# Expert products of a diffusion backbone step: gated rows turned by transposing DMAs instead of TensorE, the second product four quarters behind the first

## The reference, cut to what matters

```python
D_MODEL = 1024
N_EXPERTS = 8
TOP_K = 2
EXPERT_FF = 1024
# FFN_l, odd l: top-2-of-8 SwiGLU experts; for each chosen expert e of a token
#   y += gate[e] * ((silu(h @ w1[e]) * (h @ w3[e])) @ w2[e])
# x = LayerNorm(alpha * x + gate2 * FFN_l(x * (1 + scale2) + shift2))
```

## Time and profile before

| | us |
|---|---|
| median of 3 executions | 2330.24 (2324.44 to 2332.24) |
| the profiled execution | 2327.33 |
| its span, first to last instruction | 2325.5 |
| expert part, first `up` to last `down` | 1735.7 to 2289.2 |

### The profile page before, as it was taken

How to read it: one execution, slowest core, us unless ns; L and a number is a source line. 1 busy time by engine, 2 the same in 40 slices (tenths; PEclk the granted TensorE clock), 3 DMA queues, 4 the chain that set the end, 5 groups by cost and what they waited for, 6 DMA issues and landing times.

```text
span 2325.5 us, 54083 instructions
## 1 busy us (share of the span) xinstructions
PE 2102.1 (90%) x22914; PEld 1290.5 (55%) x22914; DVE 1440.9 (62%) x1790; ACT 1268.3 (55%) x1652; POOL 751.1 (32%) x545
## 2 busy tenths in 40 slices
PE   4999787978989999999899878878969999999998
PEld 3666456855565555555667558744644444444443
DVE  3362665668262121215547667586379999999997
ACT  3533554556444242424544675465278777777773
POOL 0322215443314343433232226433122333333332
PEclk8999899988999999999999999998979999999999
DMA  9443681020212222134331000020286779993106
GB/s 291 139 136 104 218 275 45 4 59 4 77 54 76 87 70 93 61 101 114 120 111 56 3 11 3 8 55 23 73 290 199 236 236 315 300 342 109 37 20 234
DMA packets 246504, 278.45 MB, mean 120 GB/s; under 512 B 61346, under 2 KB 221966, under 8 KB 246160
## 3 DMA queue, kind: packets, MB, share of 16 engines
q1 hardware_dynamic: 237200, 252.51, 34.6%
q0 software_dynamic: 5984, 20.97, 2.4%
q10 hardware_dynamic: 3103, 1.85, 0.3%
HBM read 360.50 MB, written 29.11 MB: 168 GB/s over the span
## 4 chain that ended last, share of the span: by engine, by line
PE 75%; DVE 9%; ACT 8%; issue 3%; DMA 2%; POOL 2%; SPq 1%; DVEq 0%; ACTq 0%; POOLq 0%
PE ps L2332 74%; DVE arena L1693 1%; ACT mix L1476 1%; DVE arena L1697 1%; DMA wbuf<-in_w_mod 1%; DVE small L1921 1%; DVE mix L1693 1%; SPq L731 1%; DMA const<-in_w_mod 1%; PE ps L3099 1%; DVE hT L1693 1%; ACT arena L1186 1%; ACT hT L1482 1%; POOL extra L922 1%; DVE const L1693 1%
## 5 line engine op out<-in xcount | busy, mean ns | idle before, releaser
L2332 PE MATMUL ps<-hT,mix 128*128 128x512 f16 (+2 forms) x3024 | 376.7, 287 | 24.8 <-DVE hT L1693 11.8
L2332 PE MATMUL ps<-w,xgT 128*128 128x512 f16 x1632 | 365.1, 380 | 4.0 <-DVE w L2239 4.0
L2332 PEld LDWEIGHTS ps<-hT,mix 128*128 128x128 f16 x3024 | 227.1, 99 | 172.7 <-issue 21.8
L2239 DVE SCALAR_TENSOR_TENSOR w<-wst,w 128x2048 f16<-128x2048 f32 x136 | 312.2, 2334 | 5.9 <-ACT w L1573 5.9
L1049 POOL TENSOR_TENSOR a<-aval,a 128x256 f16<-128x256 f32 x68 | 163.4, 2402 | 360.6 <-ACT a L1617 360.6
L2332 PEld LDWEIGHTS ps<-w,xgT 128*128 128x128 f16 x1632 | 157.3, 98 | 182.3 <-ACT xgT L1587 4.2
L1573 ACT ACTIVATE w<-wst 128x2048 f16<-128x2048 f32 x136 | 251.7, 1900 | 2.2 <-DMA xs_rows<-htok,slot_i 2.1
L2332 PE MATMUL ps<-mix 128*128 128x512 f16 (+5 forms) x1856 | 204.0, 287 | 7.2 <-ACT mix L1267 5.7
L2332 PE MATMUL ps<-hT,arena 128*128 128x128 f16 (+1 forms) x1440 | 199.4, 299 | 0.0
L2332 PE MATMUL ps<-w2m,aT 128*128 128x512 f16 x816 | 188.9, 382 | 3.1 <-DVE aT L2266 3.1
L2245 DVE SCALAR_TENSOR_TENSOR w2m<-wst,w2m 128x2048 f16<-128x2048 f32 x68 | 156.3, 2299 | 25.2 <-ACT w2m L1581 24.2
(11 more groups left out here) (360 smaller groups left out, 3482.3 us busy)
## 6 DMA issues: line engine op xcount, KB each, us to landing
wst<-in_moe_w SPq DMA_DIRECT2D x204, 1024.0 KB
wbuf<-in_w_mod SPq DMA_DIRECT2D x40, 1024.0 KB
wbuf<-in_ffn_w SPq DMA_DIRECT2D x33, 1024.0 KB
wbuf<-in_w_in SPq DMA_DIRECT2D x20, 1024.0 KB
xs_rows<-in_table SPq DMA_DIRECT2D x17, 512.0 KB, 6.2
wbuf<-in_w_out SPq DMA_DIRECT2D x32, 256.0 KB
ys_rows<-yb POOLq DMA_DIRECT2D x16, 512.0 KB, 4.3
mix<-in_w_mod SPq DMA_DIRECT2D x1, 4096.0 KB
```

What stands on the lines that cost most here:

```text
L2239: v_.scalar_tensor_tensor(out=q[1], in0=staged(s, p), scalar=WS, in1=q[0], op0=ALU.mult, op1=ALU.subtract).then_inc(sg["m_lo13"], 1)
L2332: return mm_(o, w, x, start=first, stop=last, skip_group_check=True)
```

## The change

All of it is in the expert part:

- `turn_a` and DVE's copy are gone. SP issues one transposing DMA a quarter (`turned(s)`, 128 KB, from `a16` to `aT`, both in SBUF) at the end of its turn s + 1, once `a16` of quarter s is whole (`m_alo`). It goes into the same queue as the weights.
- `a16` and `aT` have four buffers each (two and three before).
- `down(s)` comes in turn s + 4 on PE, not s + 2, and waits for the DMA (`at_in`).
- `upper2` and `lower2` come a turn later; the halves of w2 have three buffers, not two.
- Sums alternate by tile between banks 6, 7 and banks 2, 3, so that `down` of a new tile waits for the emptying of two tiles back.
- The emptying and POOL's store come two turns later.
- All ten gathers come behind POOL's loop; before, four of them came ahead of the last subtraction.
- `last_rows` comes two turns later, and two semaphores give way to a count of `m_hot`.

```diff
-        w2m = [over(f"w2m_{i}", [P, 2048], a) for i, a in enumerate((ADDR["xT"] + 32768, ADDR["wbuf"] + 16384))]
+        w2m = [over(f"w2m_{i}", [P, 2048], a) for i, a in
+               enumerate((ADDR["xT"] + 32768, ADDR["wbuf"] + 16384, ADDR["const"] + 4 * CONST_AT["hg"][0]))]
...
-            for s in range(MS):
+            def turned(s):
+                sp.wait_ge(sg["m_alo"], s + 1)
+                if s >= 4:
+                    sp.wait_ge(sg["m_down"], s - 3)
+                sp.dma_start_transpose(aT[s % 4][:, :].rearrange("p (c n) -> p c n", n=P),
+                                       a16[s % 4][:, :, :].rearrange("p i n -> p (i n)")).then_inc(at_in[s % 4], 16)
+
+            for s in range(MS + 1):
                 if s % MQ == 2 and 2 <= s // MQ + 1 < MT:
...
+                if s:
+                    turned(s - 1)
...
-                if s == MS - 2:
-                    pool.wait_ge(ys_out[0], 16 * (MT // 2))
-                    pool.wait_ge(ys_out[1], 16 * (MT // 2))
-                    pool.wait_ge(sg["m_lo13"], 2 * MS)
-                    pool.wait_ge(sg["m_up"], MS - 2)
-                    for t in range(2):
-                        gather(t)
-            for t in range(2, TT):
+            pool.wait_ge(ys_out[0], 16 * (MT // 2))
+            pool.wait_ge(ys_out[1], 16 * (MT // 2))
+            pool.wait_ge(sg["m_lo13"], 2 * MS)
+            pool.wait_ge(sg["m_up"], MS - 2)
+            for t in range(TT):
                 gather(t)
...
-                if 0 <= s - 1 < MS:
-                    upper2(s - 1)
+                if 0 <= s - 2 < MS:
+                    upper2(s - 2)
...
-                if 0 <= s - 2 < MS:
-                    dve.wait_ge(sg["m_turn"], s - 1)
-                    if s - 2 >= 3:
-                        dve.wait_ge(sg["m_down"], s - 4)
-                    v_.tensor_copy(aT[:, (s - 2) % 3, :], bank[2 + s % 2].bitcast(F16)[:, 0:512]).then_inc(sg["m_at"], 1)
...
-                pe.wait_ge(sg["m_at"], s + 1)
+                pe.wait_ge(at_in[s % 4], 16 * (s // 4 + 1))
                 pe.wait_ge(sg["m_lo2"], s + 1)
-                if q == 0 and j:
-                    pe.wait_ge(sg["m_yact"], j)
-                    pe.wait_ge(sg["m_ydve"], j)
+                if q == 0 and j >= 2:
+                    pe.wait_ge(sg["m_yact"], j - 1)
+                    pe.wait_ge(sg["m_ydve"], j - 1)
...
-            for s in range(MS + 2):
+            for s in range(MS + 4):
                 if s < MS:
                     up(s)
-                if s == MS:
+                if s == MS + 2:
                     last_rows()
-                if 0 <= s - 2:
-                    down(s - 2)
-                if 0 <= s - 1 < MS:
-                    turn_a(s - 1)
+                if 0 <= s - 4:
+                    down(s - 4)
```

More of the change, by code:

```diff
@@ L365, in backbone_kernel @@
         sgate = over("sgate", [P, 2, 256], SPARE + 4096)
-        aT = over("aT", [P, 3, 512], ADDR["va"], F16)
+        aT = [over(f"aT{i}", [P, 512], ADDR["va"] + 1024 * i if i < 3 else ADDR["states"] + 2048, F16) for i in range(4)]
         aval = over("aval", [P, 2, 256], ADDR["va"] + 3072)
-        a16 = over("a16", [P, 2, 2, 256], ADDR["lbt"], F16)
+        a16 = [over(f"a16_{i}", [P, 2, 256], a, F16) for i, a in
+               enumerate((ADDR["lbt"], ADDR["lbt"] + 1024, ADDR["states"], ADDR["states"] + 1024))]
         id16 = over("id16", [P, P], ADDR["revb"], F16)
@@ L533, in backbone_kernel @@
         xg_in = [sem(f"xg_in{i}") for i in range(2)]
+        at_in = [sem(f"at_in{i}") for i in range(4)]
         yg_in = [sem(f"yg_in{i}") for i in range(TT)]
@@ L549, in backbone_kernel @@
         w13p = [[h.rearrange("p (k n) -> p k n", k=KT) for h in halves(w13[i][:, :], 4096, 4096)] for i in range(3)]
-        w2p = [[h.rearrange("p (t n) -> p t n", t=2) for h in halves(w2m[i][:, :], 2048, 2048)] for i in range(2)]
+        w2p = [[h.rearrange("p (t n) -> p t n", t=2) for h in halves(w2m[i][:, :], 2048, 2048)] for i in range(3)]
         bank = [ps[:, b // 2, (b % 2) * 512:(b % 2) * 512 + 512] for b in range(8)]
@@ L1039, in gather @@
                                             bounds_check=MT * P - 1, oob_is_err=False).then_inc(yg_in[t], 16)
-            for s in range(MS):
-                if s >= 6 and s % MQ == 2:
-                    j = (s - 6) // MQ
+            for s in range(MS + 1):
+                if s >= 8 and s % MQ == 0:
+                    j = (s - 8) // MQ
                     pool.wait_ge(sg["m_yact"], j + 1)
@@ L1585, in _ @@
             act.wait_ge(sg["x1_out"], 16 * (TT - 1))
-            act.wait_ge(sg["m_xt"], 1)
+            act.wait_ge(sg["m_hot"], 2)
             a.activation(xgT[:, 0, 0:KT, :], ps[:, 2].rearrange("p (k n) -> p k n", k=KT), ACT.Copy).then_inc(sg["m_xhi"], 1)
             upper13(1, (1,))
-            for s in range(MS + 3):
-                if s >= 6 and s % MQ == 2:
-                    j = (s - 6) // MQ
+            for s in range(MS + 5):
+                if s >= 8 and s % MQ == 0:
+                    j = (s - 8) // MQ
                     act.wait_ge(sg["m_down"], MQ * (j + 1))
```

45 lines of the change are left out of this document (18 added, 27 removed).

## The result

The changed kernel takes 2336.95 us (median of 20 executions, 2328.86 to 2347.35), the one before, on the same chip, 2330.36 (20 executions, 2324.44 to 2337.72): ratio 1.0029, 95% interval 1.0020 to 1.0039. It is 6.6 us slower where 15.5 were forecast. The time lies in the forecast range; the forecast itself is over twice too large.

The account below looks back on a forecast made before the run. PE was taken as the bound, DVE 0.5 us behind; 2315.6 us without DMA trouble, plus 23.4 lateness and 2 for the clock, gave 2341.0 of span, plus 4.7 made 2345.7. Forecast range 2334 to 2357 (0.50); 8 in 10: 2320 to 2358.

Parts of the forecast that it names:

- the price c = 2.0 us of a transposing DMA: Time each 128 KB turning DMA takes from the weights' queue: 1.5 us gap per DMA plus 2.1 / 4 by bytes.
- the edits that were said to cost nothing: Third w2 buffer, later upper2, two pairs of banks: claimed to cost nothing, since they only loosen waits.
- Without DMA trouble: Whole span if the new DMAs delay nothing: 2325.5 - 6.3 - 13.6 + 8 + 2 = 2315.6 us.
- The start: First quarters of the expert part: up(5) starts at 1770.3 and not 1776.56, 6.3 us sooner.
- The end: After up(67), whose start is L: PE starts gathered rows at L + 25, 8 us more, plus 2 for the lower clock.
- 6.5 to land: At the end, landing time in us of the gathers, which bring PE's gathered rows to L + 25.
- As if it waited for everything ahead to land: SP's issue of the 512 KB transposing DMA rows_of took 8.33 us, against 2.47 with an idle queue.
- Rival 1: Turning DMA costs in proportion to its bytes, c = 0.6 to 0.9: 2324 us; chance 0.20.
- The spare time: At quarter 47's last w1 and w3 piece, weights have 14.8 us to spare before up(47) needs them.
- the run-in of tiles 6 and 7: Their train, 12 DMAs and 24 us longer, runs into tile 9's; the shift becomes 8.6 us at c = 2.0.
- 4.1 for one more DMA behind it: down(42), ahead of up(47), waits for its own DMA one w2 piece later: 8.9 us against 4.8, so 4.1 more.
- Rival 5: Expert part: PE is let go but ACT and DVE set the pace, 13.6 us gain lost: 2338 or more; chance 0.07.

Follow-up runs that it names:

- e3: Changed kernel without turning DMAs and SP's wait for POOL's subtraction after quarter 3, w2 of quarter s fetched in turn s, not s - 1: 2322.61 us.
- d3: Kernel before plus two transposing DMAs of 64 KB a quarter from turn 6 on, results unused: 2332.96 us.
- e1: Changed kernel with the turning DMAs left out from quarter 4 on, SP still waiting for the subtraction: 2325.46 us.
- e2: Changed kernel without turning DMAs and SP's wait for POOL's subtraction after quarter 3, w2 still fetched a turn ahead: 2319.0 us.
- e4: Changed kernel with all 68 turning DMAs, w2 of quarter s fetched in turn s and quarter s - 2 turned in turn s: 2334.56 us.
- e5: Changed kernel with eight of SP's last ten loads (four rowg, four xr) moved earlier into the loop: 2331.31 us, ratio 1.0001 to the kernel before.
- c1: Changed kernel with e4's order on SP and e5's early loads: 2325.26 us, ratio 0.9975 to the kernel before.

## Why the prediction came out as it did

**Two steps failed: the price c = 2.0 us of a transposing DMA, and the edits that were said to cost nothing.** The runs show c = 0.6, and 9.4 us lost in the queue by SP's order. The errors have opposite signs, so that 2336.95 lies between 2334 and 2357 is luck.

**Without DMA trouble it was right.** It had 2315.6 - 2325.5 = -9.9; e3, which has no such trouble, is at -9.0. PE's quarter 7.99 to 7.77: exact. The start: 6.3 forecast, 8.3 measured. The end: in these terms +5.0 forecast (L + 25, 2 for the clock, `last_rows` at L + 12.95), +8.1 in e3. Two misses of 2 and 3 us with opposite signs, so the total is near by luck too.

**The end, step by step.** The first gather at L + 17.2 came at L + 16.3 in after. From the store's issue to the first gather 6 us were taken; it was 5.3 in after and 9.6 in e3 (2270.27 to 2279.86), which is e3's miss. What failed in after is "6.5 to land": that number was read where SP's loads were already in. The prediction says that SP's loads are released at the same moment as the store, and then prices only the store with it. The gathers took 13.9, and `xr`, which the prediction never looks at, 15.3.

**The price of a transposing DMA was three times too large.** c = 2.0 was forecast, 0.6 measured. The gap in the earlier trace rows is real and comes back in after (39 GB/s at 2057), but only with some of the DMAs, and the price goes with the bytes (d3). "As if it waited for everything ahead to land" went from one case of 512 KB to a rule for 128 KB; SP sat in the issue of a turning DMA for 1.2 us on an idle queue, for 2.1 to 2.5 between 2015 and 2100 and for 4.2 at most, not for the 5 to 10 of such a rule. Rival 1, the price in proportion to the bytes (0.6 to 0.9), had the right c. What the Trainium skill says (Advanced Engine Details and Errata, section X-Bar Transpose (TRN2): as fast as ordinary DMAs) would be, as an estimate, 0.35 for 128 KB at the 373 GB/s of rows 4, or 0.4 at the 335 of e1; the runs show half as much again. The sentence that the prediction takes from the Trainium skill's page DMA: Bandwidth & Descriptors, section Rules for kernel authors, that a transpose next to ordinary DMAs needs nothing, stands there in a row on transposes that corrupt each other, and is no statement on price.

**From c to the lateness, the prediction was too lenient.** By its own steps c = 0.6 gives 2320 to 2324. Measured are 2337. The spare time is what failed. It was 14.8 us (13.7 by the packets: 397.8 - 379.3 - 4.8), less 3.5 because PE comes sooner by 16 x 0.22, and the 6 us by which SP comes later were set against 7 us of slack in the queue. That slack wasn't there. In e3 the spare is 380.4 - 363.3 - 4.8 = 12.3, much as forecast. In e1, with the new order and still without the traffic, `up(47)` is at 2266.72 - 12.95 - 20 x 7.77 = 2098.4, T + 381.0, and ACT starts on its w3 piece at 2090.67, T + 373.3; 4.8 go to ACT and DVE, and 2.9 are to spare. In after ACT starts on that piece at T + 387.3:

```profile
2090.67 1.91 ACT L1583 ACTIVATE w<-wst 128x2048 f16<-128x2048 f32 x1 [1.09 <-DMA wst<-in_moe_w]
```

```profile
2108.69 1.91 ACT L1582 ACTIVATE w<-wst 128x2048 f16<-128x2048 f32 x1 [1.22 <-DMA wst<-in_moe_w]
```

A shift of 14.0 less 2.9 is 11.1 late, and 3.1 for the lower clock make 14.2. The body of after is 14.4 longer than that of e3. That the sum fits so well is luck in part, as the waits that PE shows are for xgT and aT and not for the weights; that the spare was 3 and the shift 14 stands on rows. The 8.6 that the prediction has for the run-in of tiles 6 and 7 can't be worked out again from the figures it gives.

**"The other edits cost nothing: they only loosen waits"** was half right. `lower2` a turn later holds SP's w2 fetch, and with it the w1 and w3 pieces behind it. With no traffic in the queue that costs the body nothing (e1, e2 and e3 have one body), but 9.4 us of spare time; with the traffic it costs 2.5 to 4.8 us of the body (after against e4, e5 against c1). The wait on POOL's subtraction, at which the prediction looked, is the small one: 25.4 us.

**Where PE waits.** Forecast for quarters 44 to 47, for w or aT. It waited at `down(39)` for aT and at `up(44)` for xgT. The fetch of input rows stands in the same queue and nobody had priced it.

**The sum, term by term.** Forecast, over the kernel before: -9.9 without trouble, +25.4 for the queue, 15.5. Measured from T on: -9.0 (e3), +14.4 in the body, +0.8 in the end, +6.2. Nearly all of the miss of 9.3 is the queue's term in the body, 25.4 against 14.4: the shift of the train 16.6 too large (30.6 against 14.0), 4.1 for one more DMA behind it that didn't add, 1.1 too little for the clock, and the spare 8.4 too large (11.3 against 2.9), which hid 8 of it; these come to 11.2 where 11.0 are to be explained. Rival 5 (ACT and DVE set the pace) is refuted in the steady state, 7.77, but its mechanism is there in the recovery: once late, they catch up by 0.3 a quarter only (SP's turning DMAs, which follow them, come every (2227.94 - 2138.43) / 12 = 7.46 us where PE takes 7.77). That ACT's waits in tile 7's train at 1956 are still felt at tile 11 would follow, but no run shows it.

## What to carry to other kernels

When the bounding engine gets faster, ask whether its supply can follow. In e3 it did, by 16.0 of 17.4 us. One piece fetched behind a step that now comes a turn later took 9.4 of them away, without a trace in PE's waits until other traffic came. So an order that costs nothing alone is still to be priced as spare time, and every item of the queue, small ones too, is to be asked when it is needed. A price read off one large DMA is a price by bytes until two sizes have been seen; two small ones in place of one tell it in a single run. And a load that nobody waits for yet is still traffic: eight loads two to three turns earlier, with w2 and the turning DMA in another order, made a kernel that is 0.4% faster than before out of one that is 0.3% slower.

## What was not expected of the hardware

- Transposing DMAs of 128 KB inside SBUF, in a loaded queue, cost the weights 0.6 us each; 131 KB of weights at 335 GB/s take 0.4. Two of 64 KB cost about what one of 128 KB does (last w3 packet +11.4 and +9.4 us, ratios not to be told apart).
- The drop to 39 GB/s at such a DMA comes with some and not with others. What decides it stays open.
- The same DMA lands in 2.4 us on an idle queue and in 9.8 on a full one. A second queue for it, on ACT, was not tried.
- Ten gathers of 512 KB landed in 5.8 to 6.5 us each (median), in 13.9 beside ten plain loads of the same size. Where the loads came beside the store ahead of them instead (e3), the store held them up for 9.0 us and not 4.8.
- The part ahead of T, the same code in all kernels, ended up to 13 us apart (T at 1710.6 in d3, 1724.0 in e2), twice the effect that was to be measured.
